# First weight tiles of a stage side by side, a spare weight buffer, and norm sums as narrow columns, in a two-layer hybrid backbone

## What is computed

```python
D_MODEL, SEQ, CTX_LEN, DEPTH, D_FF = 1024, 512, 256, 2, 4096
def rms_norm(x, g):
    y = xf * lax.rsqrt(jnp.mean(xf * xf, axis=-1, keepdims=True) + NORM_EPS)
    return (y * g.astype(jnp.float32)).astype(x.dtype)
def sq_relu_mlp(h, w1, w2):
    return jnp.square(jax.nn.relu(h @ w1)) @ w2
...
for l in range(DEPTH):
    m = (silu_c @ w_mod[l] + b_mod[l])[:, None, :]
    sh1, sc1, gt1, sh2, sc2, gt2 = jnp.split(m, 6, axis=-1)
    h = rms_norm(x, g_pre_mix[l]) * (1.0 + sc1) + sh1
    y, yc = token_mixer(h, hc, p, rope_hd, rope_mla, not last)
    x = x + gt1 * rms_norm(y, g_post_mix[l])
    h = rms_norm(x, g_pre_mlp[l]) * (1.0 + sc2) + sh2
    x = x + gt2 * rms_norm(sq_relu_mlp(h, w_mlp1[l], w_mlp2[l]), g_post_mlp[l])
    # the context stream (xc, hc, yc) alike, and not in the last layer's MLP
```

## Time and profile before

| | us |
|---|---|
| median of 3 runs | 2324.39 (2322.61 to 2325.31) |
| the profiled execution, its own time | 2323.33 |
| its span in the trace | 2321.5 |
| mean granted TensorE clock | 0.974 of full |
| PE busy | 2164.8 |
| PEld busy | 1761.0 |
| DVE busy | 959.0 |
| POOL busy | 804.5 |
| ACT busy | 672.5 |

### The profile page before, as it was taken

One profiled execution on the slowest core, in us unless ns is written; L12 is line 12 of the kernel. 1 busy time (PEld: TensorE's weight loads), 2 busy tenths in 40 slices (PEclk: granted clock), 3 DMA queues, 4 the chain that ended last, 5 costly groups with the idle time before them and its releaser, 6 DMA issues.

```text
span 2321.5 us, 44921 instructions
## 1 busy us (share of the span) xinstructions
PE 2164.8 (93%) x19332; PEld 1761.0 (76%) x19332; DVE 959.0 (41%) x1442; ACT 672.5 (29%) x1186; POOL 804.5 (35%) x566
## 2 busy tenths in 40 slices
PE   5999899979898999999999899989989988999997
PEld 3888477658776888888888678847759866888886
DVE  3002355476644622414142510335486646352452
ACT  3110366642312211102111321046642323221221
POOL 3333243032144223232332543235213154444444
PEclk9999999989999999999999999999989999999998
DMA  7221200120022122222223331120120033333331
GB/s 268 83 73 55 73 2 2 61 74 4 25 70 100 55 64 64 63 63 63 63 63 136 100 119 54 38 74 1 61 73 4 12 93 119 99 94 95 93 97 63
DMA packets 45433, 163.23 MB, mean 70 GB/s; under 512 B 5505, under 2 KB 5505, under 8 KB 45025
## 3 DMA queue, kind: packets, MB, share of 16 engines
q1 hardware_dynamic: 44480, 158.29, 21.2%
q0 software_dynamic: 800, 2.69, 0.3%
HBM read 158.86 MB, written 2.10 MB: 69 GB/s over the span
## 4 chain that ended last, share of the span: by engine, by line
PE 83%; DVE 8%; ACT 4%; issue 2%; DMA 1%; POOL 1%; SPq 1%; DVEq 0%; ACTq 0%; POOLq 0%
PE ps L1489 79%; PE ps L1812 3%; DMA flat<-wmod_dram 1%; DVE part_h L1089 1%; DVE hT L1082 1%; ACT flat L795 1%; PE ps L2080 1%; DVE part_h L1358 0%; DVE flat L1473 0%; POOL xT L572 0%; POOL flat L562 0%; ACT flat L958 0%; DVE flat L1282 0%; ACT flat L959 0%; DVE flat L1291 0%
## 5 line engine op out<-in xcount | busy, mean ns | idle before, releaser
L1489 PE MATMUL ps<-part_hi,wparts 128*128 128x512 f32 (+1 forms) x3072 | 825.2, 355 | 20.4 <-DVE part_h L1089 7.4
L1489 PEld LDWEIGHTS ps<-part_hi,wparts 128*128 128x128 f32 x3072 | 548.6, 191 | 111.6 <-DVE part_h L1089 12.2
L543 POOL TENSOR_TENSOR wparts<-flat,wparts 128x1024 fp32r<-128x1024 f32 x184 | 446.8, 2428 | 524.6 <-ACT wparts L1004 518.9
L1489 PE MATMUL ps<-part_h,wparts 128*128 128x512 f32 (+1 forms) x1536 | 544.1, 354 | 0.0
L1489 PE MATMUL ps<-flat 64*64 64x32 f32 (+8 forms) x8200 | 420.9, 258 | 27.8 <-DVE flat L1303 10.6
L1489 PE MATMUL ps<-part_mlp,wparts 128*128 128x512 f32 (+1 forms) x1536 | 414.1, 357 | 15.0 <-DVE part_h L1089 9.1
L1489 PEld LDWEIGHTS ps<-flat 64*64 64x64 f32 (+4 forms) x8200 | 323.7, 142 | 112.6 <-issue 75.0
L1489 PEld LDWEIGHTS ps<-part_h,wparts 128*128 128x128 f32 x1536 | 295.1, 192 | 39.9 <-issue 1.6
L1004 ACT ACTIVATE wparts<-flat 128x1024 fp32r<-128x1024 f32 x112 | 118.8, 1061 | 695.0 <-PE ps L1489 695.0
L1489 PEld LDWEIGHTS ps<-part_mlp,wparts 128*128 128x128 f32 x1536 | 274.6, 190 | 58.8 <-POOL wparts L543 10.1
L1489 PE MATMUL ps<-part_lo,wparts 128*128 128x512 f32 (+1 forms) x768 | 272.2, 354 | 0.0
(11 more groups left out here) (210 smaller groups left out, 2052.8 us busy)
## 6 DMA issues: line engine op xcount, KB each, us to landing
flat<-w_dram SPq DMA_DIRECT2D x128, 512.0 KB, 3.6
flat<-wmod_dram SPq DMA_DIRECT2D x88, 512.0 KB, 5.6
flat<-win_dram SPq DMA_DIRECT2D x40, 512.0 KB, 3.6
flat<-wout_dram SPq DMA_DIRECT2D x16, 512.0 KB, 3.7
hT<-wmod_dram SPq DMA_DIRECT2D x8, 512.0 KB, 7.7
xT<-xT_dram SPq DMA_DIRECT2D x8, 384.0 KB, 6.6
flat<-rope_dram SPq DMA_DIRECT2D x2, 1024.0 KB, 5.5
out_dram<-xT SPq DMA_DIRECT2D x8, 256.0 KB, 2.1
```

Source lines behind the costliest of these rows:

```text
L543: pool.tensor_tensor(wlo[q % 2], src, whi[q % 2], ALU.subtract).then_inc(s_used[q], 1)
L1489: return pe.matmul(out, lhsT, rhs, start=start, stop=stop)
```

## The change

1. `product` can take several tiles and works through them k by k. The first group of a stage goes side by side in this way: two tiles at the input projection of layer 0, three at that of layer 1 (its first eight tiles have 512 columns, and the third tile has a half bank of PSUM of its own), and two at the first group of each MLP. Further tiles go one by one as before.
2. There is a third buffer for split weights, `wspare`. The third tile of the input projection uses it, and twelve of the sixteen tiles of an MLP group rotate over three buffers. GpSimd makes both parts for three tiles of an MLP group; ScalarE makes the high part of tile n once tile n - 3 is done.
3. The norm sums come as narrow columns: for each k and 128 tokens one matmul with the squares as weights and one column of ones. `token_sums` on VectorE is gone. At the start of layer 1 VectorE adds squares 4 and 5, and 6 and 7, and TensorE sums six tiles, not eight.
4. The tail rows' eight slabs have memory of their own and are loaded behind the output projection's weights. Both rows are made ahead of the norm sums.
5. `post` scales VectorE's own three tiles into PSUM and adds from there, in two column spans where there are 768 columns; each waits for the add before it.
6. TensorE's loops over the MLP and over the first eight input tiles are written out.

Core of the diff (index arithmetic and renamed arguments are left out):

```diff
+SPARE = 2
+IN_SLOT = (0, 1, SPARE) + tuple((n - 3) % 2 for n in range(3, NZ))
+MLP_SLOT = (0, 1, SPARE) * 4 + (0, 1, 0, 1)
+MLP_AFTER = (None,) * 3 + tuple(n - 3 for n in range(3, 14)) + (12, 13)
+POOL_HI = 3
...
+        PAIRED = (4, 6)
+        def acc(n):
+            return 1 + (n + 1) // 2 + (len(PAIRED) if n > 4 else 0)
+        def in_bank(l, n):
+            return 512 if l == LAST and n == 2 else n % 2 * 1024
...
-                stream(wmod_d, (MOD_FROM[l] + MOD_MIX) * SLOTS, MOD_TAIL * SLOTS)
+                for x in range(2):
+                    sp.wait_ge(s_y[x], answered(l, STEPS))
+                for k in range(MOD_TAIL * SLOTS):
+                    sp.dma_start(tail_slabs[k], wmod_d[(MOD_FROM[l] + MOD_MIX) * SLOTS + k, :, :]
+                                 ).then_inc(s_mod[2 + k // SLOTS], 16)
...
+                        if k == 6:
+                            sp.wait_ge(s_tile[3], 1 + TILES * l + T_MLP + 4 * (FFG - 1) + 3)
...
+            def in_splits(l):
+                for n in range(NZ):
+                    if n < 2:
+                        pool.wait_ge(s_tile[2 + n], TILES * l + 1)
+                    elif n == 2:
+                        pool.wait_ge(s_modmm, next_done(1) if l else MOD_FIRST)
+                    else:
+                        m = n - 3 if n < 5 else n - 2
+                        pool.wait_ge(s_tile[m % SLOTS], TILES * l + m // SLOTS + 2)
+                    split(n % SLOTS, F_IN[l] + n // SLOTS, IN_SLOT[n])
...
+            def mlp_splits(l):
+                done = TILES * l + T_MLP + 1
+                with pool.Fori(0, FFG) as i:
+                    ch.enter(i, POOL_HI)
+                    for n in range(2 * KT):
+                        q, slot = n % SLOTS, MLP_SLOT[n]
+                        src = slab[:, q * SLAB:(q + 1) * SLAB]
+                        if n < POOL_HI:
+                            if slot == SPARE:
+                                pool.wait_ge(s_modmm, tail_done(l, 1))
+                            pool.wait_ge(s_slab[q], (i * 4 + (F_MLP[l] + 1)) * 16)
+                            pool.wait_ge(s_tile[3 if slot == SPARE else 2 + n], i * 4 + (done - (1 if slot == SPARE else 0)))
+                            pool.sem_inc(s_sawslab, 1)
+                            ch.link(pool.tensor_copy(whi[slot], src))
+                        else:
+                            pool.wait_ge(s_whi, i * (2 * KT - POOL_HI) + ((2 * KT - POOL_HI) * FFG * l + n - POOL_HI + 1))
+                        pool.tensor_tensor(wlo[slot], src, whi[slot], ALU.subtract).then_inc(s_used[q], 1)
+                    ch.leave(FFG)
...
+                        if n >= POOL_HI:
+                            m = MLP_AFTER[n]
+                            act.wait_ge(s_slab[q], i * 64 + 16 * (F_MLP[l] + n // SLOTS + 1))
+                            act.wait_ge(s_tile[m % SLOTS], 1 + i * 4 + (TILES * l + T_MLP + m // SLOTS + 1))
+                            nc_.activation(whi[MLP_SLOT[n]], slab[:, q * SLAB:(q + 1) * SLAB], ACT.Copy).then_inc(s_whi, 1)
...
-            def token_sums(n, t):
...
+                own_at = (0, 3328)
+                if which == 3 and l < LAST:
+                    dve.wait_ge(s_modrow, MOD_FROM[l] + MOD_REST + 1)
+                def scaled_tile(k, a, b, out):
+                    if which == 1:
+                        return V.tensor_tensor(out, yT[:, k, a:b], rs[:, a:b], ALU.mult)
+                    return V.scalar_tensor_tensor(out=out, in0=yT[:, k, a:b], scalar=gains[:, l, which, k, a // LAT:a // LAT + 1],
+                                                  in1=rs[:, a:b], op0=ALU.mult, op1=ALU.mult)
+                own = []
                 for k in range(KT):
...
                     if k in ADDED:
+                        if which == 1:
+                            ins = scaled_tile(k, 0, t, yT[:, k, 0:t])
+                        else:
+                            for s, a, b in segs(l, True):
+                                ins = scaled_tile(k, a, b, yT[:, k, a:b])
                         ins.then_inc(s_scaled, 1)
                     else:
+                        if own:
+                            dve.wait_ge(*summed(l, which // 2, own[-1]))
+                        own.append(k)
+                        for s, a, b in segs(l, True):
+                            ins = scaled_tile(k, a, b, ps[:, own_at[s]:own_at[s] + b - a])
                         ch.link(ins)
...
+                        for s, a, b in segs(l, True):
+                            ins = V.tensor_tensor(xv[:, k, a:b], xv[:, k, a:b], ps[:, own_at[s]:own_at[s] + b - a], ALU.add)
+                        ins.then_inc(s_xup, 1)
...
+                    for n, k in enumerate(PAIRED):
+                        dve.wait_ge(s_sq, SQ * l + k + 2)
+                        V.tensor_tensor(sq[:, k, :], sq[:, k, :], sq[:, k + 1, :], ALU.add).then_inc(s_acc, 1)
...
                 if ready is None:
+                    (o, q, slot, fill), = tiles
+                    pe.wait_ge(s_used[q], fill + 2)
                     for a, b in spans:
                         for k in range(KT):
...
+                            ins = part(o, slot, k, a, b)
+                    ins.then_inc(s_tile[q], 1)
                 else:
                     for k in range(KT):
                         pe.wait_ge(ready[0], ready[1] + k)
...
+                        for o, q, slot, fill in tiles:
+                            if k == 0:
+                                pe.wait_ge(s_used[q], fill + 2)
+                            for a, b in spans:
+                                ins = part(o, slot, k, a, b)
+                            if k == KT - 1:
+                                ins.then_inc(s_tile[q], 1)
...
             def tile_sums(l, which, first, last):
+                end = PAIRED[-1] + 1 if which == 0 else KT
+                nb = NB if which == 0 or l < LAST else NBL
                 for k in range(first, last):
                     pe.wait_ge(s_sq, SQ * l + which * KT + k + 1)
...
+                    for b in range(nb):
+                        ins = mm(ps[:, NS + b:NS + b + 1], sq[:, k, b * P:(b + 1) * P], ones[:, 0:1],
+                                 k == 0 and b == 0, k == end - 1 and b == nb - 1)
+                if last == end:
+                    ins.then_inc(s_ssq, 1)
...
+            def tail_row(l, n):
+                pe.wait_ge(s_mod[2 + n], 16 * SLOTS * (l + 2))
+                modulate(tail_slabs[4 * n:4 * n + 4], 1 + n, False)
...
+                first = 2 if l < LAST else 3
+                pe.wait_ge(s_ev, 1 + 60 * l)
+                product(pre_hi[0], pre_lo, t, (s_hlo, 16 * l + 1),
+                        *((in_bank(l, n), n, IN_SLOT[n], fills[0]) for n in range(first)))
+                for n in range(first, QUERY):
+                    win_tile(n, t)
...
-                ring_row(1)
+                for n in range(MOD_TAIL):
+                    tail_row(l, n)
                 tile_sums(l, 2, 0, KT)
-                ring_row(4)
                 spread_root(l, 2)
                 pe.wait_ge(s_modrow, MOD_FROM[l] + MOD_REST)
                 mod_columns(tail_rows, 2, COL_TAIL)
...
+                for i in range(FFG):
+                    first = 0
+                    if i == 0:
+                        first = 2
+                        pe.wait_ge(s_ev, 1 + 60 * l + NZ + KT)
+                        product(pre_hi[2], pre_lo, t, (s_hlo, 16 * l + 9),
+                                *((k * 1024, k, MLP_SLOT[k], fills[0]) for k in range(2)))
+                    for k in range(first, KT):
+                        pe.wait_ge(s_ev, 1 + i * KT + 60 * l + NZ + KT + k - 1)
+                        product(pre_hi[2], pre_lo, t, None,
+                                ((k % 2) * 1024, k % SLOTS, MLP_SLOT[k], i * 4 + fills[0] + k // SLOTS))
                     for k in range(KT):
...
+                        pe.wait_ge(s_ev2, 1 + i * KT + 32 * l + max(k - 1, 0))
+                        product(h1_hi, h1_lo, t, (s_h1, i * KT + 32 * l + 2) if k == 0 else None,
+                                (2048 + (k % 2) * 1024, k % SLOTS, MLP_SLOT[KT + k], i * 4 + fills[0] + 2 + k // SLOTS))
```

More of the change, by code:

```diff
@@ L545, in splits @@
[L545 to L555 removed]
+                pool.wait_ge(s_slab[q], (fill + 1) * 16)
@@ L700, in root @@
                 act.wait_ge(s_ssq, n + 1)
[L701 removed]
+                nc_.activation(rcol[:, 0:nb], ps[:, NS:NS + nb], ACT.Sqrt,
                                scale=1.0 / DM,
```

144 lines of the change are left out of this document (46 added, 98 removed).

## The result

The changed kernel takes 2293.88 us (median of four runs, 2287.18 to 2297.6), 0.9868 of the kernel before, 95% interval [0.9853, 0.9884]; the same kernel measured a second time (e11) gave 2293.49 and 0.9868 [0.9853, 0.9883]. That is 30 us where 36.8 were predicted, inside the range. The profiled execution of after is the fastest of its four: 2287.18, span 2285.2. I compare stages, cut at the starts of ScalarE's norm roots.

A forecast was written before the change was run, and what follows sets the result against it. TensorE, busy 93% of the span, was taken as the bound, with gains only where it waits or follows VectorE in four ramps. Terms of 36.8 us off 2323.3 gave 2286.5, about 2287.5 by the median; range 2277 to 2299.

The forecast's parts named there:

- Input projection, layer 0: Second tile hides in the ramp, 5.7 us less after 0.8 for the clock; a 1.09 us wait goes, 1.1 less.
- MLP, layer 0: Ramp begins 1.25 us earlier and takes 17.4 us, not 21.8; 1.7 booked for the clock; 11.6 us less.
- Input projection, layer 1: Ramp begins 3.15 us earlier, three tiles side by side, new 2.1 us wait for GpSimd; 9.5 us less.
- MLP, layer 1: Two tiles side by side end at 1956.8, before 1963.0; 1.7 us booked for the clock; 4.5 us less.
- later: MLP after its ramp: tiles keep their time, layer 1's turns lose three quarters of 2.7 us; 2.0 us less.
- Last post: VectorE's last three adds, reading PSUM, are blocked less beside GpSimd; 2.4 us less, bounds 0 and 3.2.
- The 1.7 us of lower clock: Cost of one 3.4 us half-rate stretch in a ramp; counted 0.8 at layer 0's input projection, 1.7 in the others.
- rival C: No lower clock in any ramp, so 5.9 us come back, perhaps 3 more: 2279 us; chance 0.17.
- B: Ramps stay at the lower clock, two more 3.4 us stretches in each of four, 13.6 us: 2301; chance 0.15.
- D: GpSimd's third split locks VectorE out in the ramps, adds of squares too, some 15 us lost: 2302; chance 0.06.
- a sign of being wrong: In the changed trace, ramps longer than 17.4 us with stretched VectorE operations would show the prediction wrong.
- E: Slower: fetching TensorE's written-out MLP stalls dense tiles; 2332 us at 0.35 us a tile; chance 0.04.

The follow-up runs named there:

- e11: The changed kernel as it is, measured a second time with no edit: 2293.49 us, 0.9868 of the kernel before.
- e1: Changed kernel with the three norms' narrow sums made wide again (ones as weights) and `token_sums` back: 2288.5 us, 0.9852 of the kernel before.
- e10: Changed kernel without the pair adds of squares at layer 1's input projection, so TensorE sums all eight squares, narrow: 2303.42 us, 0.9911 of the kernel before.
- e6: Changed kernel with VectorE's own three tiles scaled and added in SBUF, not over PSUM: 2305.17 us, 0.9916 of the kernel before.
- e5: e1 with root and reciprocal taken over the whole wide row, no `token_sums`, small root or spread: 2296.92 us, 0.9879 of the kernel before.
- e7: Changed kernel with groups 1 to 3 of TensorE's MLP in a loop again, group 0 written out: 2295.91 us, 0.9875 of the kernel before.

## Why the prediction was right, and which step failed

Direction, size and range were right, by 6 us too hopeful. Before against after and e11, in the prediction's own steps:

- *Input projection, layer 0* (-6.8): IN 0 took 7.4 and 6.9 less. That this is so near is in part luck. From the root to the pair's last evacuation it is 4.0 us less (e11: 5.1), and with the wait of 1.09, which is gone, the fifth tile leaves 5.8 us earlier after the root (59.7, before 65.5); the other 1.6 lie behind the part that was changed. The ramp took 20.1 us, not 18.6, since two pairs and not one were blocked (in e11 one). No lower clock came in the ramp.
- *MLP, layer 0* (-11.6): SUMS 0 and MLP 0 together took 6.3 (e11: 7.6) less. **This is the step that failed**, and in it the sentence that a narrow k takes 1.42 and "nothing is gained there". The ramp began 28.35 us after the root before it (709.55 to 737.90), where it had begun after 23.81 (721.52 to 745.33): +4.5 instead of -1.25, because seven of eight k ran mostly at the lower clock, 1.2 GHz, and took 2.42, and the spread after them 2.93, where it had taken 1.60. The 2.42 are the narrow form's; the 2.93 came in e1 too, behind wide sums. I had read 1.42 off a single row of two k at full clock. The ramp itself was as predicted: 17.4 us.
- *Input projection, layer 1* (-9.5): SUMS 1a and IN 1 took 7.2 (7.0) less. The wait for `wparts` was 2.32, predicted 2.1. From ramp to tile four 22.9 us passed (1310.57 to 1333.44), 6.8 less than before (29.7), predicted 6.4 less with the clock. The 3.15 promised ahead of the ramp did not come, it began 0.9 later after the root than before: narrow sums again. The pair adds that I had costed at 1.5 took 4.65 us for two beside GpSimd's splits, ahead of them an operation on four columns took 2.33 (elsewhere 0.16), and in e11 TensorE waited 1.71 and 0.32 for them. They are still worth 5 to 6.5 (e10), because two k fewer were two of 2.56 each.
- *MLP, layer 1* and *later* (-4.5, -2.0): together 6.5 (8.1) less. The `part_lo` waits are all gone, 2.7 and not 2.0.
- *Last post* (-2.4): 2.2 (1.7) less, and e6 gives 2.6 to 3.1. All three adds took 0.69, as the Trainium skill's rule on "Who interferes with whom" (page "SBUF — State Buffer") had it; the trace agrees. The bound was right, the place too narrow: the same relief at layer 1's start is worth 5 to 7 us more, since there the pair adds wait behind it.

Sum of these: 29.6 us (e11: 31.3), against 36.8. The other 6.7 us (3.5) by which the profiles differ lie in stages that the change hardly touches: 1.6 ahead of the first root, which do not repeat (e11: 0.4 more than before), and 5.2 (3.9) in REST 0 and 1, whose cause no run tested. That the span of the profiled execution fell by 36.3 us, almost the 36.8, is luck: the medians differ by 30.

The 1.7 us of lower clock that I booked in each ramp did not come, as rival C had it: TensorE ran the pairs and the three tiles at 1.00, but for the first 0.5 us at layer 1's MLP, the tail of the low clock from the sums (its first matmul, at 1919.53, took 0.76). C's time did not come: a busy TensorE held the upper level in the ramps and lost it in the narrow sums. But the pair ended 3.9 us behind the ramp, not 2.1 (61.48 to 65.37, 755.3 to 759.27): the last two k arrive 1.2 us apart (2.42 for two pairs) and the two tiles need 2.08 for each. One error covered the other. B is refuted; in e5 a ramp did begin at the lower clock, behind 6.00 us of idleness. D held in one ramp of four, for 2.7 us, a sign of being wrong that did come, and in the adds of squares: in the other ramps the splits were done in time. E is refuted by e7; its count of 6,144 matmuls was wrong as well, since a tile of layer 1 has 24 and not 48, which makes 4,608.
